# Gathered expert rows of a two-layer block: v rows fetched 32 places behind u rows, part of them summed by VectorE

## What is computed

```python
def block(t):                                   # t: 128 tokens x 1024
    q = (t @ wq).reshape(PEER_BLOCK, PEER_HEADS, 2, PEER_DQ // 2)
    s1 = jnp.einsum('thd,nd->thn', q[:, :, 0], k1).astype(jnp.float32)
    s2 = jnp.einsum('thd,nd->thn', q[:, :, 1], k2).astype(jnp.float32)
    v1, i1 = lax.top_k(s1, PEER_TOPK)
    v2, i2 = lax.top_k(s2, PEER_TOPK)
...
    score, ci = lax.top_k(cand, PEER_TOPK)      # expert numbers from i1, i2, ci
...
    act = jax.nn.gelu(jnp.einsum('thkd,td->thk', u_tab[expert], t))
    return jnp.einsum('thk,thkd->td', g * act, v_tab[expert]).astype(t.dtype)
```

## Time and profile before

| | |
|---|---|
| median of 3 runs | 4361.85 us (4344.37 to 4363.55) |
| profiled execution | 4348.94 us, of it span 4347.0 us |
| busy, share of the span | TensorE 83%, VectorE 50%, ScalarE 19%, GpSimd 28% |
| DMA over the span | 765 MB, 176 GB/s on the mean |
| gathered rows | 1024 of 512 KB, from about 2590 us on |
| L2591, TensorE, v rows | 2048 matmuls, 1031.1 us, 655 ns each |
| L2668, VectorE, u rows | 512 dot products, 622.5 us, 1221 ns each |

### The profile page before, as it was taken

The page is one execution under the profiler, slowest core; times in us unless marked ns, Lnnn a source line. Parts: engine busy times, 40 slices in busy tenths (PEclk is TensorE's granted clock), DMA queues, the critical chain, the costliest instruction groups (busy, mean ns, idle before and its releaser), DMA issues.

```text
span 4347.0 us, 33067 instructions
## 1 busy us (share of the span) xinstructions
PE 3596.0 (83%) x10942; PEld 1813.3 (42%) x10942; DVE 2153.0 (50%) x4711; ACT 845.3 (19%) x1796; POOL 1226.4 (28%) x1151
## 2 busy tenths in 40 slices
PE   8778998999997989939999974668776877776877
PEld 4334554444453564426644563334232333232322
DVE  0547523100013567966525448863686876433442
ACT  1224422000032221132211223011121221111111
POOL 0200000000000000000001013453787777777774
PEclk9876999999999989969999987889898998988988
DMA  3340021222211112200222256774999999999996
GB/s 152 138 150 1 1 97 49 77 77 77 97 58 49 63 54 104 76 34 34 75 76 97 104 196 214 258 248 160 385 338 348 342 365 359 355 370 369 353 377 263
DMA packets 171912, 765.16 MB, mean 176 GB/s; under 512 B 19256, under 2 KB 19256, under 8 KB 160224
## 3 DMA queue, kind: packets, MB, share of 16 engines
q0 software_dynamic: 157904, 580.06, 36.2%
q1 hardware_dynamic: 13824, 182.97, 11.5%
q10 hardware_dynamic: 16, 0.02, 0.0%
HBM read 744.08 MB, written 18.89 MB: 176 GB/s over the span
## 4 chain that ended last, share of the span: by engine, by line
PE 49%; DVE 20%; issue 8%; DMA 5%; POOL 4%; ACT 2%; another core or an unknown queue 1%; POOLq 0%; DVEq 0%; ACTq 0%
PE ps L252 13%; PE ps L258 9%; PE ps L2591 8%; DVE arena L2668 5%; PE ps L1327 5%; PE ps L1385 5%; DVE arena L1471 4%; POOL arena L2638 4%; DMA arena<-in_pu,arena 3%; PE ps L1609 2%; PE ps L220 2%; DMA arena<-in_pv,arena 2%; PE ps L1596 1%; PE ps L831 1%
## 5 line engine op out<-in xcount | busy, mean ns | idle before, releaser
L2591 PE MATMUL ps<-arena 128*128 128x512 f32 x2048 | 1031.1, 655 | 385.0 <-issue 163.9
L2591 PEld LDWEIGHTS ps<-arena 128*128 128x128 f32 x2048 | 404.9, 206 | 991.1 <-issue 786.8
L2668 DVE CUSTOM_DVE_ANT_0 arena<-arena 128x1024 f32<-128x1024 f32 x512 | 622.5, 1221 | 387.8 <-DMA arena<-in_pu,arena 350.2
L252 PE MATMUL ps<-arena 128*128 128x512 f32 (+1 forms) x1768 | 755.0, 587 | 31.5 <-ACT arena L2157 24.4
L2638 POOL DMA_INDIRECT arena<-in_pu,arena x512 | 559.2, 1092 | 419.8 <-issue 96.5
L2638 POOL DMA_INDIRECT arena<-in_pv,arena x512 | 557.5, 1089 | 196.3 <-issue 136.0
L258 PE MATMUL ps<-arena 128*128 128x512 f32 (+2 forms) x1408 | 527.7, 536 | 3.1 <-DVE arena L1300 0.9
L252 PEld LDWEIGHTS ps<-arena 128*128 128x128 f32 x1768 | 337.2, 192 | 434.8 <-issue 429.7
L258 PEld LDWEIGHTS ps<-arena 128*128 128x128 f32 x1408 | 268.2, 191 | 262.8 <-issue 220.4
L220 PE MATMUL ps<-arena 128*128 128x128 f32 (+1 forms) x1062 | 191.4, 314 | 203.0 <-ACT arena L1686 59.8
L263 POOL TENSOR_TENSOR arena<-arena 128x1 f32<-128x1 f32 (+7 forms) x38 | 61.4, 1617 | 1012.6 <-DVE arena L675 427.7
(11 more groups left out here) (334 smaller groups left out, 3120.8 us busy)
## 6 DMA issues: line engine op xcount, KB each, us to landing
arena<-in_w_in SPq DMA_DIRECT2D x27, 2048.0 KB, 9.6
arena<-in_w_ada SPq DMA_DIRECT2D x12, 2048.0 KB, 8.1
arena<-in_w_ff_in SPq DMA_DIRECT2D x8, 2048.0 KB, 7.8
arena<-in_w_ff_out SPq DMA_DIRECT2D x8, 2048.0 KB, 8.1
arena<-in_w_pq SPq DMA_DIRECT2D x8, 2048.0 KB, 8.1
aside<-arena POOLq DMA_DIRECT2D x20, 512.0 KB, 6.8
arena<-in_w_at SPq DMA_DIRECT2D x4, 2048.0 KB, 8.4
arena<-in_w_o SPq DMA_DIRECT2D x4, 2048.0 KB, 8.0
```

Source lines behind the costliest of these rows:

```text
L252: x = t.matmul(PS[:, b, 0:n], hT[:, k, i * 128:(i + 1) * 128], w[:, k, :], start=k == 0, stop=k == nk - 1)
L2591: x = t.matmul(PS[:, b + c, :], DG[n % 4], row(f)[:, 512 * c:512 * c + 512], start=j == 0, stop=j == 127)
L2668: v.tensor_tensor_reduce(row(f), row(f), TT[i], 1.0, 0.0, ALU.mult, ALU.add, DOT[i % 2][:, j:j + 1]).then_inc(*pe.V.step("dot", 128 * i + j))
```

## The change

The list `FETCH` becomes even: from u row 32 on u and v rows alternate, a v row always 32 behind, and 33 v rows stand behind the last u row. The seven places serve the first 164 rows instead of 144. Of tile 0, the v rows with an odd j from place 72 of the list on, that is j = 21, 23 up to 127, 54 rows, are no longer multiplied on TensorE: VectorE scales the row with the coefficient and adds it to a sum in the PSUM banks 6 and 7 (`SUMS0`), which tile 1's sums use later. At tile 0's end VectorE weighs and adds that sum too (two operations), and TensorE's first v row of tile 1 waits until both sums have been read. The diagonals have a count of their own, since 54 of them are gone.

```diff
+        BEHIND = 32
...
-            goal = 0 if n_ < 64 else (n_ - 64) // 4 if n_ < 128 else 16 + (n_ - 128) * 5 // 4 if n_ < 512 else 512
+            goal = n_ - BEHIND if n_ < 512 else 512
...
-        FROM = 144
+        FROM = 164
...
+        SHARE = 72
+
+        def on_vector(i, j):
+            return i == 0 and j % 2 == 1 and NUMBER["pv", i, j] >= SHARE
+        DIAGONALS = [(i, j) for i in range(4) for j in range(128) if not on_vector(i, j)]
+        DNUMBER = {x: n for n, x in enumerate(DIAGONALS)}
+        SUMS0 = PS[:, 6:8, :].rearrange("p a n -> p (a n)")
...
+                    if not on_vector(i, j):
+                        k = DNUMBER[i, j]
+                        last = j == (126 if i == 0 else 127)
+                        if n == 128:
+                            t.wait_ge(*pe.V.at("y", 0))
+                        t.wait_ge(*fetched(f))
+                        t.wait_ge(*pe.A.at("dg", n))
+                        for c in range(2):
+                            x = t.matmul(PS[:, b + c, :], DG[k % 4], row(f)[:, 512 * c:512 * c + 512], start=j == 0, stop=last)
+                        x.then_inc(*pe.P.step("add", n))
...
+                    elif on_vector(i0, j0):
+                        g.wait_ge(*pe.V.at("added", 128 * i0 + j0))
...
-                if f == ("pv", 0, 24):
+                if f == ("pv", 0, 80):
...
+                if f and tab == "pv" and on_vector(i, j):
+                    v.wait_ge(*fetched(f))
+                    if not on_vector(i, j - 2):
+                        v.wait_ge(*pe.A.at("sc", 0, 3))
+                        pe.V.own(v).tensor_scalar(SUMS0, row(f), GS[i][:, j:j + 1], None, ALU.mult).then_inc(*pe.V.step("added", 128 * i + j))
+                    else:
+                        pe.V.own(v).scalar_tensor_tensor(out=SUMS0, in0=row(f), scalar=GS[i][:, j:j + 1], in1=SUMS0, op0=ALU.mult, op1=ALU.add
+                                                         ).then_inc(*pe.V.step("added", 128 * i + j))
...
+                    if i == 0:
+                        v.tensor_tensor(YV, SUMS0, LATE[0], ALU.mult).then_inc(*pe.V.step("y", i))
+                        pe.V.own(v).tensor_tensor(XHR, XHR, YV, ALU.add).then_inc(*pe.V.step())
```

20 lines of the change are left out of this document (9 added, 11 removed).

## The result

The changed kernel takes 4370.62 us (median of 11 runs, 4355.38 to 4373.5); the kernel before, on the same chip, 4347.82 (11 runs). The ratio is **1.0038, interval 1.0021 to 1.0056**: slower, by less than the 0.5% that the prediction called "no change", but more than nothing. The medians themselves are 22.8 us apart, and the ratio's interval stands for 9 to 24 us.

What follows compares the result with a forecast made beforehand. It took TensorE's query products, then VectorE to row 287, then row delivery (DMA 95 or 96% busy) as bounds. Terms -24 + 25 + 2 + 6 - 18 + 11 = +2 us gave 4351 or 4364; forecast 4358 us, range 4315 to 4398.

Steps and rivals of the forecast that it cites:

- no change: Whole kernel: forecast 4358 us, a difference under 0.5% (22 us) from the kernel before; chance 0.47.
- The front, the 24 us ahead: Row 37 to the last query product: product ends at about 3049 us, kernel 24 us ahead at row 167.
- Rows 168 to 287: Behind the query products: VectorE ends last with 30 additions of 1.32 us; 208 us, 25 us more.
- the 0.95 that it named as a sign of being wrong: VectorE's stretch behind the last query product: a DMA share of 0.95 would mean VectorE's work is hidden and the kernel faster.
- Tile 0's end and rows 288 to 571: Two more VectorE operations at tile 0's end, +2 us; then 142 dot products instead of 127, mostly hidden, +6 us.
- The late stage: Rows 572 to 1023 without the end: TensorE with 17 v rows fewer catches up sooner, -18 us.
- The end: Behind the last u row: 33 v rows instead of 18, last u row 15 places earlier, +11 us.
- TensorE is the late bound: Rival, late rows: TensorE fills the stretch, all 43 us come, -31 us in sum, 4318 or 4331 us; chance 0.29.
- VectorE becomes the bound, slower: Rival, rows 168 to 287: additions of 1.9 us or longer waits, +34 us in sum, 4383 or 4396 us; chance 0.24.
- The rows ahead don't come: Rival, front: v rows at 3.78 us each, nothing ahead, +26 us before the late gain; slower side, 0.24 together.

Runs made afterwards that it cites:

- e1: Changed kernel with the new order only, every v row of tile 0 back on TensorE: 4374.83 us, ratio 1.005 to the kernel before.
- e2: Changed kernel with only the front's 24 VectorE additions, the 30 in rows 168 to 287 back on TensorE: 4342.95 us, ratio 0.9982 to the kernel before.
- g4: Changed kernel with only the front's 24 additions, run once more on another chip: 4345.02 us, ratio 0.998 to the kernel before.
- e8: Changed kernel with VectorE's additions cut to 8 of 1024 columns: 4341.28 us, ratio 0.9984 to the kernel before.
- e5: Kernel before with half the v-row matmuls of tiles 2 and 3 left out, on the fast chip: 4259.14 us, ratio 0.9998.
- h1: Changed kernel with 12 diagonals in turn instead of 4, made by ScalarE: 4371.31 us, ratio 1.002 to the kernel before.
- h4: Changed kernel with additions only up to place 167, 18 v rows at the end, tokens in PSUM, four diagonals: 4351.38 us, ratio 0.9972 to the kernel before.
- e3: Changed kernel with 18 v rows instead of 33 behind the last u row: 4353.26 us, ratio 1.0004 to the kernel before.

## Why the prediction came out as it did

- **The front, the 24 us ahead: right in size, and in part by luck.** -23.0 us measured. The front was better than forecast (TensorE 91 us busy in the first stretch, 1 of 21 v rows at 3.78 us), and the last query product ended at 3037 us, not 3049. The forecast got its 24 us by setting the end of that product, 3049, against "row 167 was done at 3073 us". But 3073 us is when gather 187 started; the kernel before had used row 167 at 3051.8 us, so by the forecast's own end only some 3 us would have been left. The trace has row 167 used at 3030.5 us now, 21 us ahead, and not behind the last product at all. What made the lead is that GpSimd came out of its last long wait earlier (gather 164 at 3019.05 us for 3039.78), and from there both kernels issue at the gathers' own pace. The two errors cancel. e1 adds what the prediction did not say: without the additions in the front the order alone would have lost 10 us there.
- **Rows 168 to 287: right, +22.8 for +25.** The bound is VectorE, by the length of the additions (1.289 us for 1.29), shown by e2, g4 and e8. VectorE is 88% busy, not over 90, and the DMA share is 0.93, well above the 0.8 of the forecast and near the 0.95 that it named as a sign of being wrong; the loss is there all the same. That the addition leaves gathers alone came out as well.
- **Tile 0's end and rows 288 to 571: right, +8.6 for +8.**
- **The late stage: wrong, and this is the step that failed.** The prediction took "two fifths of GpSimd's wait, **-18 us**", on the ground that TensorE with 17 v rows fewer catches up sooner. GpSimd's wait for TensorE did shrink, by 9.8 us, and the stage by 7.0. But TensorE is not what ends last there: on the fast chip half of its matmuls left the stage as long as before (e5), and on the other chips it stayed at 604 us when twelve diagonals let TensorE go on over the pauses (h1). Nor is it GpSimd's own work alone: taking 113 us of busy time from it behind row 280 left the stage at 600 us on a chip of the result's kind (h4). What does end last there is open. A wait for an engine that has a limit on rows right behind it is worth less than its length. -7 in place of -18 gives +13 instead of +2 on the profiled execution, which is what was measured.
- **The end: right, +11.6 for +11.** From the start of the last dot product to the last sum it was 76.6 us for the forecast's 69 to 79, and that dot product came 21.5 us earlier for 22. What a short end gives back is between 5 and 15 us by e3, if the gain is real.
- **The rivals.** "TensorE is the late bound" (-31 us) is excluded by e5 on the fast chip; on the result's own kind of chip the profile (7 us for 43) and h1 speak against it, but its work was not halved there. "VectorE becomes the bound, slower" had the right mechanism, which was in the forecast's own sum, but not its size: the additions take 1.29, not 1.9 us. "The rows ahead don't come" is excluded by the profile.
- **The conclusion.** The median of 4370.6 us lies 13 us above the forecast of 4358 and inside the range; that it is so near is in part luck, since the forecast leaned on a median of three runs, 4361.9 us, and eleven runs of the kernel before have 4347.8. The step between the kernels was to be +2 us and is 9 to 24 by the ratio; the call "no change" missed a loss of 0.4% that 11 runs on each side can tell. A sum of +2 with an uncertain gain of 18 in it was +20 without it, and that should have moved the chances towards slower.

The best version found keeps the order and the front's additions and takes back the others, shortens the end and puts the tokens in PSUM, with 12 diagonals: 0.9941 on a chip like those of the result, and with four diagonals 0.9906 on the fast one.
